# SwiGLU moved behind three weight remainders at the head of the expert loop, its gate half released by itself, and the first two chunks of expert 0 loaded ahead of the last row tile

## What is computed

```python
def expert_block(args):
    idx, gate, e = args
    xb = xt[idx]
    g = jnp.minimum(xb @ w_gate[e] + b_gate[e], SWIGLU_LIMIT)
    u = jnp.clip(xb @ w_up[e] + b_up[e], -SWIGLU_LIMIT, SWIGLU_LIMIT)
    act = g * jax.nn.sigmoid(SWIGLU_ALPHA * g) * (u + 1)
    y = act @ w_down[e] + b_down[e]
    return y * gate[:, None].astype(y.dtype)
```

## Time and profile before

| | us |
|---|---|
| median of 3 runs | 2390.82 (2390.14 to 2392.67) |
| the profiled execution's own time | 2391.59 |
| its span in the profile | 2389.8 |
| TensorE matmul busy | 2272.7 (95%) |
| VectorE busy | 1504.2 (63%) |
| ScalarE busy | 1092.8 (46%) |
| GpSimd busy | 745.0 (31%) |

### The profile page before, as it was taken

How to read it: one execution, slowest core, us unless ns; L and a number is a source line. 1 busy time by engine, 2 the same in 40 slices (tenths; PEclk the granted TensorE clock), 3 DMA queues, 4 the chain that set the end, 5 groups by cost and what they waited for, 6 DMA issues and landing times.

```text
span 2389.8 us, 35306 instructions
## 1 busy us (share of the span) xinstructions
PE 2272.7 (95%) x11366; PEld 1544.4 (65%) x11367; DVE 1504.2 (63%) x1924; ACT 1092.8 (46%) x1105; POOL 745.0 (31%) x494
## 2 busy tenths in 40 slices
PE   8999999999999779899999999999999999999996
PEld 4444554787888657676666666666666666666765
DVE  3123333535344578877777777776787676787885
ACT  2112233423231146655555555655564555555654
POOL 1123121000000126363333633353444433363353
PEclk9999999999999879999999999999999999999998
DMA  5412110233333369998877878887898888788985
GB/s 199 112 27 78 44 44 10 80 97 88 95 120 121 144 229 334 336 302 294 278 262 270 299 265 309 286 281 270 295 327 262 280 289 272 267 296 287 332 304 184
DMA packets 205429, 517.97 MB, mean 217 GB/s; under 512 B 18816, under 2 KB 85888, under 8 KB 205376
## 3 DMA queue, kind: packets, MB, share of 16 engines
q1 hardware_dynamic: 189248, 470.57, 55.1%
q0 software_dynamic: 16128, 46.67, 9.0%
HBM read 480.94 MB, written 32.05 MB: 215 GB/s over the span
## 4 chain that ended last, share of the span: by engine, by line
PE 78%; DVE 11%; issue 5%; ACT 3%; DMA 2%; ACTq 1%; POOL 0%; DVEq 0%; SPq 0%; POOLq 0%
PE psum L1662 13%; PE psum L1664 11%; PE psum L1663 11%; PE psum L1485 7%; PE psum L1429 7%; PE psum L1673 5%; DVE w_lo L1225 4%; PE psum L1507 4%; PE psum L1506 4%; PE psum L1505 3%; DVE st L1253 2%; DMA ring<-in_w_down 1%; ACT w_hi L807 1%; PE psum L1591 1%; PE psum L1715 1%
## 5 line engine op out<-in xcount | busy, mean ns | idle before, releaser
L1225 DVE TENSOR_TENSOR w_lo<-ring,w_hi 128x2048 fp32r<-128x2048 f32 x384 | 865.6, 2292 | 65.8 <-ACT w_hi L807 63.5
L807 ACT ACTIVATE w_hi<-ring 128x2048 fp32r<-128x2048 f32 x384 | 723.0, 1919 | 142.7 <-DMA ring<-in_w_down 94.8
L1662 PE MATMUL psum<-w_hi,xT_hi 128*128 128x512 f32 x992 | 419.9, 423 | 62.1 <-DVE w_lo L1225 59.0
L1663 PE MATMUL psum<-w_lo,xT_hi 128*128 128x512 f32 x992 | 403.0, 406 | 0.0
L1664 PE MATMUL psum<-w_hi,xT_lo 128*128 128x512 f32 x992 | 402.8, 406 | 0.0
L601 POOL TENSOR_SCALAR pick<-iota_bf,slot_col 128x256 bf16<-128x256 bf16 x252 | 399.3, 1595 | 4.4 <-DVE slot_col L1238 4.4
L607 POOL DMA_INDIRECT xg<-h_rows,idx_new x33 | 70.0, 2121 | 833.7 <-DVE idx_new L1219 808.5
L1662 PEld LDWEIGHTS psum<-w_hi,xT_hi 128*128 128x128 f32 x992 | 193.4, 195 | 178.9 <-DVE w_lo L1225 82.2
L1662 PE MATMUL psum<-w_hi,aT_hi 128*128 128x512 f32 x544 | 228.3, 420 | 9.4 <-DVE aT_lo L1262 6.3
L1664 PEld LDWEIGHTS psum<-w_hi,xT_lo 128*128 128x128 f32 x992 | 193.3, 195 | 47.5
L1663 PEld LDWEIGHTS psum<-w_lo,xT_hi 128*128 128x128 f32 x992 | 194.5, 196 | 40.9
(11 more groups left out here) (298 smaller groups left out, 3000.4 us busy)
## 6 DMA issues: line engine op xcount, KB each, us to landing
ring<-in_w_gate SPq DMA_DIRECT2D x256, 512.0 KB, 5.0
ring<-in_w_up SPq DMA_DIRECT2D x256, 512.0 KB, 6.4
ring<-in_w_down SPq DMA_DIRECT2D x256, 512.0 KB, 6.1
ring<-in_w_in SPq DMA_DIRECT2D x44, 512.0 KB, 5.1
ring<-in_x SPq DMA_DIRECT2D x16, 512.0 KB, 3.4
ring<-in_w_in SPq DMA_DIRECT2D x6, 1024.0 KB, 7.7
vb<-oT SPq DMA_DIRECT2D x16, 256.0 KB, 10.5
ring<-in_w_oc SPq DMA_DIRECT2D x16, 256.0 KB, 3.0
```

What stands on the lines that cost most here:

```text
L807: e.activation(w_hi[:, hs, :], ring[:, slot, :], ACT.Copy).then_inc(g_hi, 1)
L1225: e.tensor_tensor(w_lo[:, hs, :], ring[:, slot, :], w_hi[:, hs, :].bitcast(F32), ALU.subtract).then_inc(g_lo, 1)
L1662: e.matmul(dst, hi, w_up, start=start, stop=False)
L1663: e.matmul(dst, hi, w_rest, start=False, stop=False)
```

## The change

In the loop VectorE's `swiglu` leaves the end of a pass and stands in the next one, behind the remainders of chunks 9, 10 and 11. `evacuate` takes the quarter tile first, then the gate half and then the up half, so that ScalarE's `sigmoid` waits for one increment of `g_ev` and not for two. ScalarE rounds chunk 9 at the end of a pass instead of at the next one's head, and chunk 14 ahead of `act_rows`; VectorE takes the remainder of chunk 14 ahead of `rest_of_act` too. Ahead of the loop, chunks 0 and 1 of expert 0 are loaded before the last row tile is written out, the remainder of chunk 8 stands ahead of the rest of the rows, and TensorE starts `first_gate_up` when the first half of the rests of the rows is there.

```diff
                 e.dma_start(out[P * t:P * t + P, :], xe[t % 2]).then_inc(x1_out[t % 2], 16)
+                if t == TT - 1:
+                    e.wait_ge(e_mm, 2 * TT)
+                    for k in range(2):
+                        load_gate_up(0, k, k, 0)
                 e.wait_ge(e_xn, t + 1)
...
-            e.wait_ge(e_mm, 2 * TT)
-            for k in range(MSLOT):
+            for k in range(2, MSLOT):
                 load_gate_up(0, k, k, 0)
...
             def sigmoid(n, hb):
-                hold(e, g_ev, 2 * n + 2)
+                hold(e, g_ev, 2 * n + 1)
...
+            round_weights(0, 8 + 1, False)
             sigmoid(0, hb0)
             with e.Fori(0, n_loop) as p:
...
-                for k in range(1, 3):
-                    round_weights(p, 8 + k, False)
+                round_weights(p, 8 + 2, False)
...
-                for k in range(3, 6):
+                for k in range(3, 7):
                     round_weights(p, 8 + k, False)
                 act_rows(p, hb, 4, 7)
-                for k in range(6, GU_CHUNKS):
+                for k in range(7, GU_CHUNKS):
                     round_weights(p, 8 + k, False)
...
                 round_weights(p, 12 + 8, False)
+                round_weights(p, 12 + 9, False)
...
             def evacuate(n, hb):
-                e.wait_ge(g_gu, 2 * n + 1)
-                e.tensor_scalar(gt[:, :], psum[:, 0:D], LIMIT, None, ALU.min).then_inc(g_ev, 1)
+                hold(e, g_gu, 2 * n + 1)
                 with e.If(hb > 0):
                     e.tensor_scalar(gtb[:, :], bank[6][:, 0:QD], LIMIT, None, ALU.min)
                     e.tensor_scalar(utb[:, :], bank[6][:, QD:2 * QD], LIMIT, -LIMIT, ALU.min, ALU.max)
+                e.tensor_scalar(gt[:, :], psum[:, 0:D], LIMIT, None, ALU.min).then_inc(g_ev, 1)
...
+            rest_of_weights(0, 8)
             rest_of_rows(1, xT_hi, xT_lo, 4)
-            rest_of_weights(0, 8)
             evacuate(0, hb0)
-            swiglu(0, hb0)
             row_numbers(2, 7)
             with e.Fori(0, n_loop) as p:
...
-                rest_of_weights(p, 8 + 1)
-                for k in range(2, 4):
+                for k in range(1, 4):
                     rest_of_weights(p, 8 + k)
+                swiglu(p, hb)
+                rest_of_weights(p, 8 + 4)
                 slots_of(p + 3, exn)
-                for k in range(4, 6):
+                for k in range(5, 7):
                     rest_of_weights(p, 8 + k)
                 rest_of_act(p, 4)
-                for k in range(6, GU_CHUNKS):
+                for k in range(7, GU_CHUNKS):
                     rest_of_weights(p, 8 + k)
...
-                swiglu(p + 1, hbn)
                 shift_rows(p, False)
...
+            swiglu(n_loop, hbe)
             rest_of_weights(n_loop, 8 + 1)
...
-                e.wait_ge(g_xlo, 2)
                 for k in range(GU_CHUNKS):
+                    if k % 4 == 0:
+                        e.wait_ge(g_xlo, 1 + k // 4)
```

More of the change, by code:

```diff
@@ L430, in _, with load_gate_up @@
                 load_item(n)
+            wg = A["w_gate"].rearrange("e (k p) n -> p e k n", p=P)
+            wu = A["w_up"].rearrange("e (k p) n -> p e k n", p=P)
+            wd = A["w_down"].rearrange("e (k p) n -> p e k n", p=P)
+            def load_gate_up(p, c0, k, ex):
+                _, slot, _, _ = chunk_at(p, c0)
+                for j, w in enumerate((wg, wu)):
+                    src = w[:, bass.ds(ex, 1), k:k + 1, :].rearrange("p e k n -> p (e k n)")
+                    e.dma_start(ring[:, slot, D * j:D * j + D], src).then_inc(g_w[slot], 16)
             for t in range(TT):
@@ L446, in _ @@
                     e.dma_start(xe[t % 2], A["x"][P * (t + 2):P * (t + 3), :]).then_inc(xe_in[t % 2], 16)
[L449 to L457, removed]
             def load_down(p, c0, c, ex):
@@ L873, in _ @@
                 round_weights(p, 12 + 8, False)
+                round_weights(p, 12 + 9, False)
             hbl = e.value_load(table[0:1, bass.ds(n_loop + (NT - 1), 1)], min_val=0, max_val=1)
             hbe = e.value_load(table[0:1, bass.ds(n_loop + NT, 1)], min_val=0, max_val=1)
-            for c in range(1, 3):
-                round_weights(n_loop, 8 + c, False)
+            round_weights(n_loop, 8 + 2, False)
             act_rows(n_loop, hbe, 0, 2)
@@ L1356, in _ @@
             hb0 = e.value_load(table[0:1, NT:NT + 1], min_val=0, max_val=1)
+            rest_of_weights(0, 8)
             rest_of_rows(1, xT_hi, xT_lo, 4)
-            rest_of_weights(0, 8)
             evacuate(0, hb0)
-            swiglu(0, hb0)
             row_numbers(2, 7)
             with e.Fori(0, n_loop) as p:
+                hb = e.value_load(table[0:1, bass.ds(p + NT, 1)], min_val=0, max_val=1)
                 hbn = e.value_load(table[0:1, bass.ds(p + (NT + 1), 1)], min_val=0, max_val=1)
                 exn = e.value_load(table[0:1, bass.ds(p + 3, 1)], min_val=0, max_val=E - 1)
-                rest_of_weights(p, 8 + 1)
-                for k in range(2, 4):
+                for k in range(1, 4):
                     rest_of_weights(p, 8 + k)
+                swiglu(p, hb)
+                rest_of_weights(p, 8 + 4)
                 slots_of(p + 3, exn)
-                for k in range(4, 6):
+                for k in range(5, 7):
                     rest_of_weights(p, 8 + k)
                 rest_of_act(p, 4)
-                for k in range(6, GU_CHUNKS):
+                for k in range(7, GU_CHUNKS):
                     rest_of_weights(p, 8 + k)
```

## The result

The changed kernel takes 2334.25 us, the median of 4 runs (2328.4 to 2339.0), against 2391.74 for the kernel before in the same rounds. The ratio is 0.9759, 95% interval 0.9735 to 0.9783, some 57.5 us. The forecast was 2324 (2309 to 2344), so the median lies 10 us above the forecast and just outside its inner band, 2314 to 2334. The execution in the profile took 2328.4, with a span of 2326.6; it is the fastest of the four, so what follows explains 63 us of its span, and the other three runs lie up to 11 us above it.

What follows compares the result with a forecast made beforehand. TensorE was taken as the bound, waiting at pass heads behind SwiGLU. 58.6 us in the loop plus 8.0 ahead of it, 66.6 in all, took the profiled 2391.6 to 2325.0, so 2324 us, range 2309 to 2344.

Steps and rivals of the forecast that it cites:

- What bounds the kernel: Expert loop: TensorE is the bound, losing 53.2 us in 34 waits, nearly all at the heads of passes.
- The loop: All 30 passes: 1371.6 us against 1430.2, 58.6 us less; passes of 40.0, 46.8, 51.65 and 44.4 us by kind.
- The seam: Head of a pass: moving SwiGLU takes 2.78 us off the 3.04 us wait; a narrow seam still waits about 0.2 us.
- The clock: Loop: with no long wait the granted clock stays at 1.00, where the mean over all passes was 0.98.
- Chunk 14 ahead: Passes with a narrow gate: 0.65 us of new wait at chunk 15, in place of 0.16 at chunk 14.
- Transfers and picks: Passes with neither product wide: 0.4 us added to each, the DMA share being 0.96 there already.
- signs of "wrong": Waits at slot_rows or for aT_lo each pass, chunk 14 landing after 15 us, or 42 us narrow passes, DMA share near 1.
- the rival of transfers: Narrow-gate passes: slipping loads or late picks make them 42 and 45.5 us, about 2352 us in all; chance 14%.
- Picks: GpSimd's picks start 12.6 us behind the head and end by 34.2, before slot_rows at 34.8: cost 0.
- The rival made of late picks: Narrow-down passes: each pick blocked 4.70 us, ending 50.2 us behind the head; 200 us slower, 2524 us; chance 3%.
- Ahead of the loop: Before the loop and at its first head: 2.1 us from an earlier gather plus 5.8 at chunk 9, about 8.0 us.
- Behind the loop: After the last pass: remainder and SwiGLU only change order, the sum stays the same, gain 0.

Runs made afterwards that it cites:

- 9 us more delay: Changed kernel with slot_col and the eight picks moved behind the remainder of chunk 15, some 9 us later in a narrow pass: 2359.37 us.
- The two runs on it: Changed kernel with the early loads of expert 0's first two chunks undone, 2330.59 us; changed kernel with TensorE's register load ahead of its gates wait, 2328.14 us.
- the second trace: The changed kernel run again with no edit: 2331.28 us, ratio 0.9753 to the kernel before.
- the swap: GpSimd's scatter(p) put ahead of gather(p + 2), in the kernel with chunk 14 behind activations, early register load and chunk 9's remainder first: 2333.45 us.

## Why the prediction was right, and where it was off

**What bounds the kernel.** Right. The seam's waits were 53.2 us, and with SwiGLU out of them they are gone; SwiGLU's move alone gives the whole gain (2324 us), and SwiGLU back brings the waits back (2396 us).

**The loop.** 1371.6 forecast, 1369.7 measured, each kind within 0.3 us. That the sum is so close is in part luck: I had charged 8.2 us for chunk 15 and 3.2 for transfers and picks, and the waits measured are 4.5 us at chunk 15 and 8.8 at chunk 14, so that one term was too large and the other too small. The terms:

- *The seam.* Forecast 0.2 us left, measured 0.03. The two rows that gave 3.44 against 3.45 us were right for the changed kernel. With SwiGLU's move alone 0.2 to 0.4 us are left at four heads, so the other parts took that away; I had counted them as nothing. The wait of 0.97 us for the round of chunk 19, gone in the changed kernel, points at the earlier sigmoid, but no run moved it by itself.
- *The clock.* Forecast 1.00 throughout, measured 1.00 in the mean of the loop, with 0.96 in a pass that waited 1.8 us.
- *Chunk 14 ahead.* I charged 0.65 us to each narrow gate, 0.5 of it new. What it cost was 0.32 us of wait in fourteen passes; undone, it gives 6.5 us of the median, 0.43 for each pass with a narrow gate. The mechanism, the activations in front of the remainder of chunk 15, is as forecast, but as a part of the change it was not worth making.
- *Transfers and picks.* I charged 0.4 us to the eight shortest passes. What they paid was late loads at chunk 14 in eleven passes, 8.8 us in all, which the passes with down alone paid too. I had taken the slowest landing from the issue, 6.9 us, and so 13.7 us behind the head as the latest; the changed kernel has landings up to 16.7. The cause, the scatters in the same stretch, stood in no term. So two of my signs of "wrong" came true in single passes (chunk 14 later than 15 us, a pass of 42.0), as far as the rival of transfers is real; it did not take every narrow pass.
- *Picks.* Forecast to start at 12.6 and end by 34.2; they started at 11.5 to 13.2 and ended at 23.7 to 29.5. Cost 0, as forecast. The bound of 34.2 had less room than it seems: it took in gather and scatter, but in the run without the scatters the eight picks alone, with the same start, ended as late as 33.3 us behind the head in the shortest passes. I had read a pick held for 7 us out of the page's rule; the longest in the changed kernel took 4.64. The rival made of late picks came true with 9 us more delay; what less delay does was not run.

**Ahead of the loop.** Here a step failed. "All else in that list is in time, so 2.1 us is the most that this gives, and I take it": the first product came 0.4 us sooner, and not by way of the gathered rows. Their transposes began 0.2 us later than before (843.08 against 842.84), and the idle time in front of the first product fell from 1.88 to 1.28, also with the loads late, so that it most likely comes of the wait for only the first half of the rests, which no run changed by itself. I read VectorE's wait for the gathered rows and did not read TensorE's row for their transposes, in the kernel before:

```profile
842.84 0.45 PE L1655 MATMUL psum<-ident,xg 128*128 128x128 f32 x1 [4.46 <-issue]
```

The two runs on it show that the loads' place gives nothing and that TensorE's own register load held the transposes. At chunk 9 I counted the whole wait of 5.81 us as given back; 2.11 stayed. I had left the 1.52 us of issue in front of VectorE's remainder as it stood; with a third register load, which the change adds, it became 2.26, and with all three behind that remainder both it and TensorE's wait went.

**Behind the loop.** Forecast 0, measured 2.1 us lost in the profiled execution and 1.4 in the second one. The terms that I compared, the remainder and SwiGLU in either order, are equal in VectorE's list; but the transposes that stood right behind the last seam before (2356.5) now wait for SwiGLU too, 3.28 us, and the product starts 9.35 us behind the seam instead of 7.91; the other 0.65 us lie in the product itself, which had a granted clock of 0.83 instead of 0.87. In the second trace that clock is 0.87 again and only the 1.4 us are lost.

**The number.** These two, 3.3 and 2.1 us, less 1.9 in the loop, make the profiled execution 3.5 us slower than forecast (2328.4 against 2325.0). The other 6 us to the median are runs whose trace was not taken. What the second trace adds: its execution took 2331.1, of which 1.9 us lie before the first seam and 1.4 in the loop. What causes the rest of the spread stays open.

## What to carry to other kernels

Ask of each part of a change by itself: here one part gave the whole gain, one took 6.5 us of it back, and the rest weighed nothing that the times can tell. When a wait goes, look what lands latest in the new schedule, and take its time from what shares the queues in that stretch, not from its median. When an instruction is put further ahead in a list, look first what it waits for: the scatters stood behind ScalarE's `ys`, and the swap only pushed the gather back. Where a row says "issue", look for a register load in that engine's own list, and move it into an earlier wait.

## What the runs showed of the hardware

- A GpSimd instruction that reads SBUF lasted 4.82 us in place of 0.91 under two VectorE subtracts with both inputs in SBUF, and 0.91 beside evictions from PSUM.
- In the stretch of the row scatters the DMA engines were 0.81 busy and moved 104 GB/s; two windows later (1010.1 to 1012.1) they moved 389 GB/s. Without the scatters chunk 14's load, issued at the same 6.4 us behind the head, landed some 3 us sooner (12.4 against 15.8 in the passes shown).
- Moving one register load ahead of a wait took 2.0 us off TensorE's way to the transposes behind its first branch. VectorE's three register loads at the loop's first entry took 2.26 us, and nothing visible once an instruction stood ahead of them.
